# Values made with tokens on the partitions, four heads at a time, in a hybrid decoder trunk; the first two gates each moved one place forward

## The chip, the core and the metric

The kernel runs on one core of one Trainium2 chip. The metric is the device time of one execution in microseconds (us). TensorE is the engine of the matmuls, VectorE, ScalarE and GpSimd work on tiles, SyncE issues most of the transfers. In the rows they are PE, DVE, ACT, POOL and SP; PEld is TensorE's weight load, and "SPq" and "ACTq" are transfers issued by SyncE and ScalarE.

## The reference

Two layers over 256 tokens of width 2048, all float32. Each layer has three branches that are mixed by gates, and a SwiGLU block behind them.

```python
proj = einsum('bld,de->ble', x, w_in[l]) + b_in[l]
q_sb, k_sb, v_sb, u_ssm, q_mem, gate_logits = split(proj, ...)   # 1024, 1024, 1024, 512, 512, 3 x 2048
sb    = stick_breaking_attention(q_sb, k_sb, v_sb)               # 8 heads of 128
p_sb  = sb @ sb_w_out[l]
g     = gelu(s5(u_ssm, ...));  a, b = split(g @ ssm_w_glu[l])
p_ssm = (a * sigmoid(b)) @ ssm_w_out[l]
p_mem = memory_attention(q_mem, mem, mem_w_kv[l]) @ mem_w_out[l]
gates = sigmoid(gate_logits)                                     # three gates of 2048
merged = gates[0] * p_sb + gates[1] * p_ssm + gates[2] * p_mem
x = layer_norm(ALPHA * x + merged @ w_o[l])
x = layer_norm(ALPHA * x + (silu(x @ w_gate) * (x @ w_up)) @ w_down)
```

For one head the attention takes weights w_t (tokens by tokens, through a sigmoid and a running product) and multiplies them with v; the matmul needs v with the key tokens on the partitions.

## The kernel before

**Precision and chunks.** Each float32 operand is split into a high part (fp32r) and the rest: `hi` is a ScalarE copy of a loaded weight (L736), `lo` a VectorE subtraction of the two (L1206). A product is hi*hi + lo*hi + hi*lo. Weights come in chunks of 1 MB (128 x 2048), in four `raw` slots filled by SyncE, and are split in halves of 128 x 1024 into four `hi` and four `lo` slots. A half's slot is free when TensorE has done the half four places back (`half_done`). Chunks are numbered through the whole program, by the table PHASES: U (the first states of a layer), BR (three branch turns of 10 chunks), BL (the last turn, 6 chunks), GLU (18), G (three merge groups of 16), WO, F0, FB, FL. On ScalarE and VectorE `split_next` (L739, L1209) stands for each chunk c and splits chunk c + 1, so both engines' queues are an order written out by hand, with their other work between.

**Two forms of product.** `product` (L1822) makes one 128-wide output with the output's columns on the partitions: a 128 x 128 block of weights is stationary, and x streams past, 512 columns (hi and lo of 256 tokens) for the hi weights (L1829), 256 for the lo weights (L1832), 16 times in a chunk. The result is [head column, token]; ScalarE takes its first 256 columns (`first_half`, L753), VectorE adds the second 256 (`take`, L1215). `group_half` (L1867) has tokens on the partitions: a block of x is stationary and 512 columns of weights stream past, three times for each block (L1854 to L1856), for two blocks of tokens, 24 matmuls in a chunk; four chunks make 512 output columns in two banks.

**A branch turn** (L2002 on TensorE, L917 on ScalarE, L1447 on VectorE) has two attention heads, one memory head and 128 SSM channels. Its chunks are q, k, v of the first head (0, 1, 2), q, k, v of the second (3, 4, 5), and k, v of the memory, u and q of the memory for the next turn (6 to 9). Between them stand small float32 products: `state_inputs` (L2019), the memory scores (L2099), z, tri, `attend` (L2071) and `state_outputs`. A scan over time runs on VectorE (`scan_states`), ten steps for each of two pairs, and ends in `state_outputs`. `v_turn` (L2064) transposes v of a head (k = 0 and 2, source v_f) and of the memory (k = 1, source vm_f) by two 128 x 128 transposes each (L2068); ScalarE copies the result (`copy_v`, L953) to v_s or vm_s. In the first turn of layer 0 eight tables are transposed as well and saved to DRAM (`table`), and ScalarE waits for these saves before it goes on to the output of the first head. Set-up work for the SSM runs on GpSimd until about that turn.

**The last turn and the merge.** In BL the places of chunks 6 to 9 are taken by the four chunks of the first gate (`first_gate`, L1995), into banks 2 and 3. Then come the GLU products in four steps t = 0 to 3 (`glu_blocks`, L2190) into the banks of GLU_BANK, steps 0 and 1 first without their last quarter, which waits for the last GELU. Then TensorE does the sb products (two chunks, banks 2 and 3), gate 1 (four chunks, banks 0 and 1), ssm (one chunk, banks 2 and 3 again), gate 2 (four chunks, banks 4 and 5) and mem (one chunk, banks 6 and 7). VectorE adds a gate's bias to its logits (`gate_logits`, L1619), ScalarE does a tanh, and VectorE's `merge(b)` multiplies the branch by it (L1630 for b = 0). Before ssm, TensorE waits for merge(0), which reads banks 2 and 3, and for the GLU's last result:

```python
branch_products("GLU", 0, GLU_SPANS, 0)                                  # L2223
pe.wait_ge(tile_out, tile_no("GLU", l, 0, 7) + 1 + TILE_CREDIT)
gate_products("GLU", 0, GLU_SPANS, 1)
pe.wait_ge(merge_step, 20 * l + 1)
pe.wait_ge(glu_lo, 4 * l + 4)
branch_products("GLU", 0, GLU_SPANS, 1)                                  # L2228
```

On VectorE merge(0) comes in the loop at L1685 behind `split_next("GLU", l, 0, 8)`, that is, behind both lo halves of chunk 9. Ahead of the first norm of each layer TensorE runs matmuls whose result nobody reads (L2297), and sixteen of that kind on ident (L1914) at the program's start.

## Time and profile before

| | |
|---|---|
| median of 3 runs | 2956.91 us (2956.4 to 2957.02) |
| profiled execution | 2957.04 us |
| its span | 2955.3 us (1.7 us lie around it) |
| TensorE, VectorE, ScalarE busy | 99%, 65%, 46% of the span |
| mean rate of the transfers | 192 GB/s |
| chain that ended last | 97% TensorE |

In the timeline a row is: start, duration, engine, line, operation, output <- input, shapes, count; in brackets the idle time ahead of it and what ended it. An x2 row holds two instructions. Starts of TensorE are measured, ends are modelled: a matmul's cost in a stream is the distance from its start to the next one's. In the view of waits a row gives who waited for whom, the total, the times and the longest, in us.

### The profile page before, as it was taken

To read this page: it belongs to the slowest core of one execution; us is meant where nothing else is said; L and a number is where in the kernel's file an instruction comes from. 1 tells how busy PE (TensorE), PEld (TensorE's weight loads), DVE (VectorE), ACT (ScalarE), POOL (GpSimd) and SP (SyncE) were. 2 spreads that over 40 slices of the span, in tenths; PEclk is the share of its full clock that TensorE was granted. 3 is DMA by queue.
4 is the path that set the end of the run, shared out by engine and by line. 5 is a ranking of instruction groups with operands and counts; after the bars stand their busy time and mean duration, and the time that the engine had idled before them with its cause. 6 is when DMAs were issued, how large, how long until landed. Compare 5 with 4: busy or idle time off the path is not lost.

```text
span 2955.3 us, 37621 instructions
## 1 busy us (share of the span) xinstructions
PE 2935.8 (99%) x14068; PEld 2449.7 (83%) x14068; DVE 1932.0 (65%) x2754; ACT 1371.5 (46%) x1646; POOL 46.6 (2%) x117
## 2 busy tenths in 40 slices
PE   8999999999999999999999999999999999999999
PEld 7888888888888888888888888888888888888887
DVE  8899755555755555555699996555666555555556
ACT  6656544444544444444466554444444444444443
POOL 5000000000000000000000000000000000000000
PEclk9999999999999999999999999999999999999999
DMA  9666565656655555555556565665656555555554
GB/s 252 194 189 179 198 205 194 207 190 212 229 191 192 187 196 185 194 189 190 191 140 170 161 188 195 203 202 198 223 172 213 185 194 189 188 195 185 189 194 142
DMA packets 390020, 568.31 MB, mean 192 GB/s; under 512 B 20408, under 2 KB 194592, under 8 KB 389024
## 3 DMA queue, kind: packets, MB, share of 16 engines
q1 hardware_dynamic: 385712, 554.77, 58.5%
q10 hardware_dynamic: 4208, 12.21, 1.1%
q8 instruction: 62, 1.02, 0.1%
q14 instruction: 38, 0.31, 0.0%
HBM read 558.81 MB, written 8.13 MB: 192 GB/s over the span
## 4 chain that ended last, share of the span: by engine, by line
PE 97%; DVE 1%; ACT 1%; DMA 0%; issue 0%; SPq 0%; ACTq 0%; DVEq 0%
PE banks L1854 26%; PE banks L1856 26%; PE banks L1855 26%; PE banks L1829 9%; PE banks L1832 4%; PE banks L1844 1%; PE banks L2275 1%; PE banks L2209 1%; PE banks L2297 0%; DMA raw<-in_w_in 0%; DVE lo L1206 0%; PE banks L1846 0%; PE banks L2028 0%; PE banks L2040 0%; PE banks L2210 0%
## 5 line engine op out<-in xcount | busy, mean ns | idle before, releaser
L1206 DVE TENSOR_TENSOR lo<-raw,hi 128x1024 fp32r<-128x1024 f32 x1014 | 1232.0, 1225 | 957.5 <-ACT hi L736 870.6
L736 ACT ACTIVATE hi<-raw 128x1024 fp32r<-128x1024 f32 x932 | 977.8, 1059 | 1163.1 <-PE banks L1856 1155.1
L1854 PE MATMUL banks<-hi,xs 128*128 128x512 f32 x2176 | 852.0, 392 | 2.4 <-DVE xs L1349 2.4
L1856 PE MATMUL banks<-hi,xs 128*128 128x512 f32 x2176 | 847.3, 389 | 0.0
L1855 PE MATMUL banks<-lo,xs 128*128 128x512 f32 x2176 | 846.9, 389 | 0.0
L1854 PEld LDWEIGHTS banks<-hi,xs 128*128 128x128 f32 x2176 | 408.5, 188 | 86.6 <-DVE xs L1349 2.9
L1856 PEld LDWEIGHTS banks<-hi,xs 128*128 128x128 f32 x2176 | 408.4, 188 | 85.2
L1855 PEld LDWEIGHTS banks<-lo,xs 128*128 128x128 f32 x2176 | 408.7, 188 | 82.9
L1829 PE MATMUL banks<-xs,hi 128*128 128x512 f32 x960 | 307.1, 401 | 0.5 <-DVE lo L1206 0.5
L1854 PE MATMUL banks<-hi,hT 128*128 128x512 f32 x704 | 274.1, 389 | 0.0
L1856 PE MATMUL banks<-hi,hT 128*128 128x512 f32 x704 | 273.9, 389 | 0.0
L1855 PE MATMUL banks<-lo,hT 128*128 128x512 f32 x704 | 273.9, 389 | 0.0
L1832 PEld LDWEIGHTS banks<-xs,lo 128*128 128x128 f32 x960 | 180.3, 188 | 42.6
L1832 PE MATMUL banks<-xs,lo 128*128 128x256 f32 x960 | 189.2, 278 | 0.0
L1856 PEld LDWEIGHTS banks<-hi,hT 128*128 128x128 f32 x704 | 132.1, 188 | 27.4
L1854 PEld LDWEIGHTS banks<-hi,hT 128*128 128x128 f32 x704 | 132.1, 188 | 27.4
L1855 PEld LDWEIGHTS banks<-lo,hT 128*128 128x128 f32 x704 | 132.2, 188 | 27.3
L1829 PEld LDWEIGHTS banks<-xs,hi 128*128 128x128 f32 x960 | 146.9, 189 | 5.9 <-issue 5.5
L748 ACT ACTIVATE hi<-raw 128x1024 fp32r<-128x1024 f32 x80 | 83.9, 1059 | 106.2 <-PE banks L1856 106.2
L1410 DVE TENSOR_TENSOR rows<-rows,banks 128x1024 f32<-128x1024 f32 (+1 forms) x98 | 109.2, 1147 | 3.3 <-PE banks L1856 3.3
L1854 PE MATMUL banks<-hi,mT 128*128 128x512 f32 x256 | 99.8, 390 | 0.0
L1856 PE MATMUL banks<-hi,mT 128*128 128x512 f32 x256 | 99.6, 389 | 0.0
(254 smaller groups left out, 2430.5 us busy)
## 6 DMA issues: line engine op xcount, KB each, us to landing
raw<-in_ffn_w_gate_up SPq DMA_DIRECT2D x176, 1024.0 KB, 5.0
raw<-in_w_in SPq DMA_DIRECT2D x156, 1024.0 KB, 5.2
raw<-in_ffn_w_down SPq DMA_DIRECT2D x88, 1024.0 KB, 4.9
raw<-in_w_o SPq DMA_DIRECT2D x32, 1024.0 KB, 5.0
raw<-in_sb_w_out SPq DMA_DIRECT2D x16, 1024.0 KB, 5.0
raw<-in_mem_w_kv SPq DMA_DIRECT2D x12, 1024.0 KB, 5.8
raw<-in_ssm_w_out SPq DMA_DIRECT2D x8, 1024.0 KB, 5.1
raw<-in_mem_w_out SPq DMA_DIRECT2D x8, 1024.0 KB, 5.1
```

The lines of the kernel that those rows point to most:

```text
L736: act.activation(hi[:, hl_slot(ph, c, h), :], raw[:, slot, h * HALF:(h + 1) * HALF], ACT.Copy).then_inc(hi_ready, 1)
L748: act.activation(hi[:, hl_slot(ph, c + 1, h), :], raw[:, slot, h * HALF:(h + 1) * HALF], ACT.Copy).then_inc(hi_ready, 1)
L1206: dve.tensor_tensor(lo[:, s, :], raw[:, slot, h * HALF:(h + 1) * HALF], hi[:, s, :].bitcast(F32), ALU.subtract).then_inc(lo_ready, 1)
L1410: dve.tensor_tensor(y2, y2, src, ALU.add).then_inc(rows_out, 1)
L1829: pe.matmul(dst[:, :], hi[:, s, k * P:(k + 1) * P], x_t[:, k0 + k, :], start=first and k == 0, stop=False)
L1832: ins = pe.matmul(dst[:, 0:T], lo[:, s, k * P:(k + 1) * P], x_t[:, k0 + k, 0:T], start=False, stop=last and k == 7)
L1844: pe.matmul(bank[base + j], hi[:, s, at[j]], x_t[:, k, :], start=k == 0, stop=False)
L1854: pe.matmul(dst, xh, hi[:, s, w], start=first, stop=False)
L1855: pe.matmul(dst, xh, lo[:, s, w], start=False, stop=False)
L1856: return pe.matmul(dst, xl, hi[:, s, w], start=False, stop=last)
L2209: pe.matmul(dst[:, :], hi[:, s, w], gT[:, k, :], start=k == 0, stop=False)
L2275: ins = pe.transpose(bank[base + q][:, k * T + m * P:k * T + (m + 1) * P], silu[:, m, (2 * q + k) * P:(2 * q + k + 1) * P], ident[:])
```

## The change

v of four heads is made at once in the second form, with tokens on the partitions: the first four heads' v by four chunks at the end of U (c = 4 to 7), the other four's in places 2 and 5 of turns 0 and 1, where v's chunks stood. VectorE's new `v_rows` adds the bias out of banks 2 and 3 into v_first or v_last, which `attend` reads. v_turn is left for vm_f alone; passes and takes for v go. In places 2 and 5 of turns 2 and 3 the first gate is made, in BL's last places the second gate, and the GLU phase has no gate 1 between sb and ssm. Banks change (BU, tables, GLU_BANK), and some set-up work moves behind U's new chunks. On SyncE, ScalarE and VectorE the order follows. The diff, cut; its hunks are those of the order tables, SyncE, ScalarE, VectorE and TensorE.

```diff
-    "U": (1, [0, 1, 2, 3], [2] * 4),
+    "U": (1, [0, 1, 2, 3] * 2, [2] * 4 + [1] * 4),
...
-    "GLU": (1, ([2, 3, 0, 1] * 5)[:18], [1] * 4 + [4] * 2 + [1] * 12),
+    "GLU": (1, ([2, 3, 0, 1] * 4)[:14], [1] * 4 + [4] * 2 + [1] * 8),
...
-GLU_SPANS = {"gate0": 0, "glu": 4, "sb": 6, "gate1": 8, "ssm": 12, "gate2": 13, "mem": 17}
+GLU_SPANS = {"gate1": 0, "glu": 4, "sb": 6, "ssm": 8, "gate2": 9, "mem": 13}
...
-GLU_BANK = (0, 1, 4, 5, 6, 7, 0, 1)
+GLU_BANK = (4, 5, 6, 7, 4, 5, 6, 7)
+TILE_AT = {0: 0, 1: 1, 3: 2, 4: 3, 6: 4, 7: 5, 8: 6, 9: 7}
+WIDE_AT = (2, 5)
...
-        BU, Z, S, VO, Y = (bank[2], bank[3], bank[4], bank[6]), bank[4], bank[5], bank[6], bank[7]
+        BU, Z, S, VO, Y = (bank[5], bank[4], bank[6], bank[7]), bank[4], bank[5], bank[6], bank[7]
...
+                for c in range(4):
+                    load_block("U", 0, 4 + c, w, 4 * c, 2 * SBW)
+                    if l == 0 and c == 1:
+                        load_ssm_rest()
+                if l == 0:
+                    sp.wait_ge(par_T, 1)
+                else:
+                    sp.wait_ge(v_ready, 2 * l)
+                load_v_bias(0)
...
+                    cols = [(w, t * 256), (w, t * 256 + SBW), None, (w, t * 256 + P), (w, t * 256 + SBW + P), None]
...
+                        if at is None:
+                            load_block(ph, i, c, w, 4 * (2 * (t % 2) + WIDE_AT.index(c)),
+                                       2 * SBW + GROUP if t < 2 else GATE_COLS)
+                        else:
+                            load(ph, l, i, c, columns(*at))
+                    if t == 0:
+                        sp.wait_ge(v_ready, 2 * l + 1)
+                        load_v_bias(1)
...
-                for c in range(4):
-                    load_gate_block("GLU", 0, GLU_SPANS, 0, 1, c)
-                    if c == 0:
-                        sp.wait_ge(attn_done, 12 * l + 15)
-                        load_bias(0, 1)
+                sp.wait_ge(attn_done, 12 * l + 15)
+                load_bias(0, 1)
                 load_branch("GLU", 0, GLU_SPANS, 0, 1)
-                sp.wait_ge(gate_in, 12 * l + 1)
-                load_bias(0, 2)
                 for c in range(4):
                     load_gate_block("GLU", 0, GLU_SPANS, 0, 2, c)
+                    if c == 2:
+                        sp.wait_ge(gate_in, 12 * l + 1)
+                        load_bias(0, 2)
                 load_branch("GLU", 0, GLU_SPANS, 0, 2)
...
+                split_next("U", l, 0, 4)
                 for k, col in enumerate((None, None, bias_col(l, 24), bias_col(l, 28))):
                     first_half("U", l, 0, k, bank[U_BANK[l][k]], done("U", l, 0, 1 if l and k < 2 else 3), col)
-                    if l == 0 and k == 1:
-                        b_blocks(0, 4)
+                split_next("U", l, 0, 5)
+                if l == 0:
+                    c_blocks(0, 1)
+                split_next("U", l, 0, 6)
+                if l == 0:
+                    b_blocks(0, 4)
+                split_next("U", l, 0, 7)
...
-                    tile(2, turn * 2 + 16)
...
-                    copy_v(0, VO, v_s, 3)
...
+                    def v_rows(g, dst, ready):
+                        dve.wait_ge(half_done, ready)
+                        dve.wait_ge(v_bias_in, 16 * (2 * l + g + 1))
+                        dve.tensor_tensor(dst[:].rearrange("p h m d -> p m h d"),
+                                          banks[:, 2:4, :].rearrange("p m (h d) -> p m h d", d=P),
+                                          v_bias[:].rearrange("p a (h d) -> p a h d", d=P)
+                                          .broadcast_to([P, TT, 4, P]), ALU.add).then_inc(v_ready, 1)
...
+                    if turn == 0:
+                        v_rows(0, v_first, chunk_no(ph, l, i, 0) * 2 + HALF_CREDIT)
...
-                    tile(2, v_f)
...
+                        if turn == 1:
+                            v_rows(1, v_last, chunk_no(ph, l, i, 6) * 2 + HALF_CREDIT)
...
-                for c in range(7, 18):
+                for c in range(7, 14):
                     split_next("GLU", l, 0, c)
                     if c == 8:
                         merge(0, 4 * l, upto("GLU", 0, 8))
-                    if c == 12:
-                        gate_logits(1, 4 * l, GATE_BANK[1], upto("GLU", 0, 12))
+                        gate_logits(1, 4 * l, GATE_BANK[1], upto("GLU", 0, 4))
+                    if c == 9:
+                        merge(1, 4 * l, upto("GLU", 0, 9))
                     if c == 13:
-                        merge(1, 4 * l, upto("GLU", 0, 13))
-                    if c == 17:
-                        gate_logits(2, 4 * l, GATE_BANK[2], upto("GLU", 0, 17))
+                        gate_logits(2, 4 * l, GATE_BANK[2], upto("GLU", 0, 13))
...
+                for c in range(4):
+                    for h in range(2):
+                        k = 4 * c + 2 * h
+                        group_half("U", l, 0, 4 + c, h, xs, k, 2, k == 0, k == KD - 2)
...
-                def first_gate(c):
+                def second_gate(c):
                     if c == 0:
-                        pe.wait_ge(bu_copied, 16 * l + 18)
+                        pe.wait_ge(tile_out, tile_no("GLU", l, 0, 0) + TILE_CREDIT)
                     for h in range(2):
                         k = 4 * c + 2 * h
-                        group_half("GLU", l, 0, c, h, xs, k, 2, k == 0, k == KD - 2)
+                        group_half("GLU", l, 0, c, h, xs, k, GATE_BANK[1], k == 0, k == KD - 2)
...
+                    def wide(c):
+                        at = 2 * (turn % 2) + WIDE_AT.index(c)
+                        if at == 0:
+                            pe.wait_ge(v_ready, 2 * l + 1 + turn // 2)
+                        for h in range(2):
+                            k = 4 * at + 2 * h
+                            group_half(ph, l, i, c, h, xs, k, 2, k == 0, k == KD - 2)
...
+                        pe.wait_ge(gelu_step, n * 5 + 1)
...
                     got(-1)
+                    pe.wait_ge(bu_copied, n * 4 + 3)
                     for t in range(TT):
                         ins = pe.matmul(S[:, t * T:(t + 1) * T], qm_f[:, t * P:(t + 1) * P], km_f[:], start=True,
                                         stop=True)
                     ins.then_inc(s_done, 1)
                     gemm(1, xs)
-                    gemm(2, xs)
+                    wide(2)
...
-                    v_turn(0, v_f, VO)
...
+                    vm_turn()
+                    wide(5)
...
-                    v_turn(2, v_f, VO)
...
                     if ks[0] == 0:
                         if t == 0:
-                            pe.wait_ge(tile_out, tile_no("GLU", l, 0, 0) + TILE_CREDIT)
-                        elif t == 1:
                             pe.wait_ge(w_ready, 8 * (l + 1) + 1)
                             pe.wait_ge(o_lo, 12 * (l + 1))
-                        elif t == 2:
+                        elif t == 1:
                             pe.wait_ge(o_lo, 12 * (l + 1) + 1)
                             pe.wait_ge(gelu_step, (4 * l + 3) * 5 + 6)
                         else:
-                            pe.wait_ge(tile_out, tile_no("GLU", l, 0, 1) + 1 + TILE_CREDIT)
+                            pe.wait_ge(tile_out, tile_no("GLU", l, 0, 2 * t - 3) + 1 + TILE_CREDIT)
...
                 pe.wait_ge(tile_out, tile_no("GLU", l, 0, 7) + 1 + TILE_CREDIT)
-                gate_products("GLU", 0, GLU_SPANS, 1)
                 pe.wait_ge(merge_step, 20 * l + 1)
                 pe.wait_ge(glu_lo, 4 * l + 4)
                 branch_products("GLU", 0, GLU_SPANS, 1)
```

## Rows read from the trace of the kernel before

**Rows 1.** The page's first part, TensorE: busy us, share, count; VectorE and ScalarE behind.

```profile
PE 2935.8 (99%) x14068; PEld 2449.7 (83%) x14068; DVE 1932.0 (65%) x2754; ACT 1371.5 (46%) x1646; POOL 46.6 (2%) x117
```

**Rows 2.** The waits of TensorE over the span: total us, times, longest.

```profile
PE banks L2133 <- ACT vm_s L956: 1.4, 1, 1.4
PE banks L1992 <- ACT b_blk L831: 1.0, 1, 1.0
PE banks L1992 <- ACT stage L913: 0.8, 2, 0.5
...
PE banks L1829 <- DVE lo L1206: 0.5, 1, 0.5
```

**Rows 3.** TensorE's timeline in the last branch turn of layer 0.

```profile
262.60 0.63 PE L1829 MATMUL banks<-xs,hi 128*128 128x512 f32 x2
...
268.17 0.59 PE L2048 MATMUL banks<-q_f,k_f 128*128 128x256 f32 x2
...
269.30 0.71 PE L1829 MATMUL banks<-xs,hi 128*128 128x512 f32 x2
...
274.97 0.38 PE L2068 MATMUL banks<-ident,v_f 128*128 128x128 f32 x2
275.19 0.60 PE L2058 MATMUL banks<-sp_t,ntri 128*128 128x256 f32 x2
...
289.70 0.48 PE L1854 MATMUL banks<-hi,xs 128*128 128x512 f32 x1
...
295.27 0.38 PE L2068 MATMUL banks<-ident,v_f 128*128 128x128 f32 x2
```

**Rows 4.** The timeline of all engines in the GLU products of layer 0.

```profile
319.79 0.66 ACT L759 ACTIVATE tmp<-banks 128x256 f32<-128x256 f32 x2 [0.38 <-PE banks L2210]
...
320.21 0.76 DVE L1219 SCALAR_TENSOR_TENSOR glu<-banks,tmp 128x256 f32<-128x256 f32 x2 [1.89 <-ACT tmp L759]
320.30 0.40 PE L2209 MATMUL banks<-gT,hi 128*128 128x512 f32 x1
```

**Rows 5.** The timeline of all engines near the end of a branch turn (the third).

```profile
242.23 1.12 DVE L1496 SCALAR_TENSOR_TENSOR scan<-scan,pw,scan_t 128x127 f32<-128x127 f32 x4
...
245.39 0.85 PE L2040 MATMUL banks<-scan,tab 128*32 128x256 f32 x12
```

**Rows 6.** The timeline of all engines at the end of the sb products of layer 0.

```profile
336.89 0.39 PE L1854 MATMUL banks<-hi,xs 128*128 128x512 f32 x1
337.10 1.06 ACT L736 ACTIVATE hi<-raw 128x1024 fp32r<-128x1024 f32 x1 [1.60 <-PE banks L1856]
...
338.19 1.23 DVE L1206 TENSOR_TENSOR lo<-raw,hi 128x1024 fp32r<-128x1024 f32 x1 [1.16 <-ACT hi L736]
...
339.33 1.21 DVE L1630 SCALAR_TENSOR_TENSOR acc<-gate,banks 128x1024 f32<-128x1024 f32 x1
```

**Rows 7.** TensorE's timeline over the ssm chunk of layer 0: its first, the next chunk's first.

```profile
358.66 0.39 PE L1854 MATMUL banks<-hi,ssmT 128*128 128x512 f32 x1
...
364.10 0.39 PE L1854 MATMUL banks<-hi,xs 128*128 128x512 f32 x1
```

**Rows 8.** The timeline of all engines in the first branch turn of layer 0.

```profile
43.53 0.63 PE L1829 MATMUL banks<-xs,hi 128*128 128x512 f32 x2
...
50.73 1.13 PE L2099 MATMUL banks<-km_f,qm_f 128*128 128x256 f32 x4
50.81 1.08 ACT L934 ACTIVATE scan<-banks 128x512 f32<-128x512 f32 x2 [1.95 <-PE banks L2028]
...
52.96 2.01 ACT L736 ACTIVATE hi<-raw 128x1024 fp32r<-128x1024 f32 x2 [0.69 <-DMA raw<-in_w_in]
```

**Rows 9.** TensorE's timeline at the program's start, the warming matmuls.

```profile
4.28 3.41 PE L1914 MATMUL banks<-ident 128*128 128x128 f32 x16
...
8.40 1.95 PE L1914 MATMUL banks<-ident 128*128 128x128 f32 x16
```

**Rows 10.** Busy time in a stretch: engines, then granted clock (PEclk), DMA share, GB/s.

```profile
88.00:92.00 4.00, 2.55 (x14) 2.08 (x13) 3.79 (x17) 1.02 (x3) 0.00 (x0) 1.00 0.72 204
```

More of the change, by code:

```diff
@@ L52 @@
 ORDER = ["U", "BR", "BL", "GLU", "G", "WO", "F0", "FB", "FL"]
-TILES = {"U": 4, "BR": 10, "BL": 6, "GLU": 8, "G": 0, "WO": 0, "F0": 0, "FB": 0, "FL": 0}
+TILES = {"U": 4, "BR": 8, "BL": 4, "GLU": 8, "G": 0, "WO": 0, "F0": 0, "FB": 0, "FL": 0}
 def _bases(per_turn):
@@ L155, in trunk @@
         region = ExitStack()
+        ahead = sb("ahead", [P, 6, 2 * T], stack=region)
+        v_last = sb("v_last", [P, 4, 2, P], stack=region)
+        region.close()
+        region = ExitStack()
         b_nat = sb("b_nat", [P, 2, 32, GC], stack=region)
@@ L184, in trunk @@
         k_f = sb("k_f", [P, T], stack=region)
-        v_f = sb("v_f", [P, T], stack=region)
+        gel_y = sb("gel_y", [P, T], stack=region)
         qm_f = sb("qm_f", [P, T], stack=region)
@@ L454, in branch_turn @@
                                  (w, (t + (3 * SBW // P + 1)) * P), (w, (t + ((3 * SBW + SSMW) // P + 1)) * P)]
-                    for c, (src, col) in enumerate(cols):
-                        load(ph, l, i, c, columns(src, col))
-                        if first and c == 1:
-                            load_ssm_rest()
+                    for c, at in enumerate(cols):
+                        if at is None:
[6 more added lines that the diff above has]
+                        load_v_bias(1)
                 if l == 0:
@@ L494, in _ @@
                 for c in range(4):
-                    load_gate_block("GLU", 0, GLU_SPANS, 0, 0, c)
+                    load_gate_block("GLU", 0, GLU_SPANS, 0, 1, c)
                     if c == 1:
@@ L926, in tile @@
                             bias = bias_col(l, bias_tile)
-                        first_half(ph, l, i, c, bank[c % 2], done(ph, l, i, c), bias, scale)
-                        if l == 0 and turn == 1 and c % 2 and c < 8:
-                            save_mem(c // 2)
+                        k = TILE_AT[c]
+                        first_half(ph, l, i, k, bank[k % 2], done(ph, l, i, c), bias, scale)
+                        if l == 0 and turn == 1 and k % 2:
+                            save_mem(k // 2)
                     def copy_bu(j):
@@ L1027, in branch_turn @@
                     out_hi(0, VO, sbT[:, bass.ds(turn * 2, 1), 0:T])
-                    copy_v(1, S, vm_s, 2)
-                    tile(5, turn * 2 + 17)
+                    copy_vm()
                     softplus(1)
@@ L1454, in tile @@
                     def tile(c, dst, scale=1.0):
-                        take(ph, l, i, c, bank[c % 2], dst[:], scale)
+                        k = TILE_AT[c]
+                        take(ph, l, i, k, bank[k % 2], dst[:], scale)
+                    def v_rows(g, dst, ready):
[5 more added lines that the diff above has]
+                                          .broadcast_to([P, TT, 4, P]), ALU.add).then_inc(v_ready, 1)
                     def scan_states(pair, first, last_):
@@ L1647, in _ @@
                 split_next("GLU", l, 0, 4)
-                gate_logits(0, 4 * l, 2, upto("GLU", 0, 4))
+                gate_logits(0, 4 * l, 2, upto("GLU", 0, 0))
                 def glu_take(t):
@@ L1684, in _ @@
                 dve.wait_ge(glu_lo, 4 * l + 4)
-                for c in range(7, 18):
+                for c in range(7, 14):
                     split_next("GLU", l, 0, c)
@@ L2062, in tri, with vm_turn @@
                                   skip_group_check=True).then_inc(tri_done, 1)
-                    def v_turn(k, src, o):
-                        pe.wait_ge(v_copied, n * 3 + (k + 1))
+                    def vm_turn():
+                        pe.wait_ge(v_copied, n + 1)
                         for t in range(2):
-                            ins = pe.transpose(o[:, t * P:(t + 1) * P], src[:, t * P:(t + 1) * P], ident[:])
+                            ins = pe.transpose(S[:, t * P:(t + 1) * P], vm_f[:, t * P:(t + 1) * P], ident[:])
                         ins.then_inc(vt_done, 1)
@@ L2073, in attend @@
                         pe.wait_ge(w_ready, n * 2 + (e + 2))
-                        pe.wait_ge(v_copied, n * 3 + (2 + 2 * e))
+                        pe.wait_ge(v_ready, 2 * l + 1 + turn // 2)
                         pe.wait_ge(o_lo, n * 3 + (e + 1))
-                        pe.matmul(VO[:, T:2 * T], v_s[:, 0, :], w_t[:, 0:T], start=True, stop=False)
-                        pe.matmul(VO[:, T + P:2 * T], v_s[:, 1, :], w_t[:, T:384], start=False, stop=True
+                        v, at = (v_first, v_last)[turn // 2], (2 * turn + e) % 4
+                        pe.matmul(VO[:, T:2 * T], v[:, at, 0, :], w_t[:, 0:T], start=True, stop=False)
+                        pe.matmul(VO[:, T + P:2 * T], v[:, at, 1, :], w_t[:, T:384], start=False, stop=True
                                   ).then_inc(attn_done, 1)
@@ L2092, in branch_turn @@
                         pe.wait_ge(tab_b_full, n * 16)
-                    got(-2)
+                    got(-1 if turn == 0 else -2)
                     state_inputs()
```

152 lines of the change are left out of this document (70 added, 82 removed).

## The prediction, made before the change was run

> **What bounds the kernel now.** The page comes first: TensorE is busy 2935.8 us of a span of 2955.3 us, VectorE 65% and ScalarE 46% of it [rows 1]. So every microsecond that TensorE issues counts, and work of the other engines counts only where TensorE waits for it. The view of TensorE's waits shows how little there is to win besides: in the part that the change touches they are 1.4 us for vm_s, 1.0 us for b_blk, 0.8 us for the table copies and 0.5 us for a lo half [rows 2]; all fall into the first branch turn of layer 0. The later branch turns have none. The change is therefore an account of TensorE's own instructions, plus the places where it sets TensorE next to work that used to be hidden. The timeline of one engine has to be read by its starts: the ends are modelled, so the cost of a matmul is the distance to the next start.
>
> **Part 1, the transposes of v, taken out.** A turn of one head's v starts at 274.97 us and the next work at 275.19 us [rows 3]: 0.22 us. There are two in a turn (k = 0 and 2 of v_turn), and 2 layers have 8 turns, so there are 16 of them: 16 x 0.22 = 3.5 us saved. All of it is on TensorE and on the path. With them go, for each head, a 256-wide pass and a copy on ScalarE and a take of about 0.38 us on VectorE (0.76 us for two such [rows 4]). I cost these at nothing: TensorE hides them, and nothing in a steady turn waits for those engines. What comes late next would be the scan: VectorE's last step ends at 242.23 + 1.12 = 243.35 us and TensorE reads it at 245.39 us [rows 5], 2.0 us of room. TensorE's turn gets about 0.7 us shorter, VectorE loses two takes, and in turns 0 and 1 it gains v_rows, a 1024-wide add out of two banks, nearest to the 1.21 us of the merge step [rows 6]. Room left: 2.0 - 0.7 + 0.8 - 1.2 = 0.9 us, so still no wait. In turn 1 v_rows stands ahead of scan steps and a take for km_f, in turn 0 behind the split of the second chunk and ahead of the scan; both queues have work of TensorE's of a whole chunk before they are needed.
>
> **Part 2, the products for v.** The number of columns is the same. A head in the old form streams 16 x (512 + 256) columns, 12288; a chunk in the new form streams 24 x 512, 12288 too, and layer by layer 8 chunks stand for 8. The form has a price, though. An old chunk runs from 262.60 to 268.17 us, 5.57 us; behind fp32 work from 269.30 to 274.97, 5.67 us [rows 3]. A chunk in the new form takes 364.10 - 358.66 = 5.44 us [rows 7], and behind fp32 work 295.27 - 289.70 = 5.57 us [rows 3]. That is 0.13 and 0.10 us less; half of the 16 chunks stand in either place: 8 x 0.13 + 8 x 0.10 = 1.8 us saved. The first gate's four chunks move into turns 2 and 3, the second gate's into the last turn, in the form that they have: nothing.
>
> **Part 3, the GLU banks.** Step t = 2 gets banks 4 and 5, which step t = 0 has just filled, where before it had free ones. It must wait until both halves are taken. Before, ScalarE starts on them at 319.79 us and VectorE's two takes run from 320.21 for 0.76 us, to 320.97 us, while TensorE starts step 2 at 320.30 us [rows 4]. So TensorE waits 0.67 us and a semaphore's way: 0.7 us, twice: 1.4 us lost. Step 3's banks are taken by the time it comes.
>
> **Part 4, the second gate no longer stands between the sb and the ssm products.** Both write banks 2 and 3, so the ssm products wait for merge(0), as before. But before, 4 chunks of the second gate covered it; now there is nothing between. What stands ahead of merge(0) on VectorE stays: the split of the chunk after next. Its second half needs the hi slot that the last sb half frees. The trace of before shows this very sequence with TensorE busy elsewhere: the matmul behind the last one of sb starts at 336.89 us; ScalarE begins the hi half at 337.10, VectorE the lo half at 338.19 and merge(0) at 339.33 us for 1.21 us [rows 6]. It is over at 340.54 us, 3.65 us after 336.89. With the way to TensorE 3.7 us, once a layer: 7.4 us lost. The lower end is merge alone, behind sb at once: 1.3 us a layer; the order in VectorE's queue rules it out, and I take 3.7. ssm also waits for glu_lo, done long before under the two sb chunks. The second logits and the tanh come behind merge(0) and are not waited for until the G loop, 5 chunks on. SyncE's queue: the ssm load now stands behind the wait for the last attention product and one bias load, the third bias load inside gate 2's loads; both conditions hold before the slots come free.
>
> **Part 5, the start of layer 0.** Four wide chunks (21.8 us) now run at 43.53 us [rows 8], ahead of the first branch chunk, and give the set-up time. The waits for the lo half (0.5 us) and for b_blk (1.0 us) [rows 2] lie behind a late VectorE and go; of the table copies' 0.8 us I let 0.3 go, since ScalarE has one pass less before them. The vm_s wait hangs on ScalarE waiting for a table save to land; I leave it. Saved 1.8 us. Two costs stand against it. The states now fill bank 5 first, which the memory scores need: the scores start at 50.73 us, while ScalarE's first two copies start at 50.81 us and take 1.08 us for both [rows 8], so the scores would wait for the first until about 51.35: 0.6 us, in this turn alone (elsewhere a half chunk lies between). And the third v chunk takes the place in SyncE's queue of the chunk that ScalarE had to wait for, until 52.96 us [rows 8]. The hi half takes 1.0 us of that 2.01 us pair and the lo half as long as that between 338.19 and 339.33 [rows 6], 1.2 us with its end, so it would be ready at about 55.2 us, while TensorE arrives at 43.53 + 2 x 5.44 = 54.4 us: 0.8 us at most, nothing if the wider rows land sooner; I take 0.4. Net: -1.8 + 0.6 + 0.4 = -0.8 us, bounds -3.7 (all four waits of [rows 2] gone, no cost) and +1.5.
>
> **Sum.** -3.5 - 1.8 + 1.4 + 7.4 - 0.8 = +2.7 us. The profiled execution took 2957.04 us, its span plus 1.7; the median of the runs is 2956.91. So 2956.9 + 2.7 = 2959.6 us, 0.09% above before. About 0.2%, 5.9 us, is what a measurement of this kernel can tell from no change.
>
> **Rivals.**
> 1. Slower: the clock falls in the new gap. Nothing in the trace of before, once it is under way, shows TensorE idle for as long as 3.7 us. At the start it shows both paces: the first 16 warming matmuls on ident take 3.41 us from end to end, the same 16 later 1.95 us [rows 9], about half the pace, the 1.2 GHz level against 2.4. One such slow stretch behind the gap costs 3.41 - 1.95 = 1.5 us, one twice as long 3 us; two layers, 3 to 6 us: 2962.6 to 2965.6. From 1.6 us a gap on, the whole is 0.2% slower. For it: the code puts matmuls that compute nothing ahead of each layer's first norm. Against it: the 1.4 us wait of [rows 2] passes without loss; the granted clock stays at 1.00 around it [rows 10]. Chance 0.14. The Trainium skill ("TensorE: Matmul & The Clock Gate", section "Why this matters for your kernels") speaks against this change here: it warns of idle gaps between bursts of matmuls, after which the clock is back at half. By that rule the gap would be followed by a slow stretch; no row of before has a gap to test it on.
> 2. The start of layer 0 is short of data: the third and fourth v chunks land 2 to 3 us late because the small SSM loads sit ahead of them. Then 2961.5 to 2963. For it: ScalarE already waits for that load [rows 8]. Chance 0.10.
> 3. The extra 21.8 us wipe out all waits of the first turn (-3.7 in place of -0.8): 2956.7. For it: VectorE and ScalarE start that turn with nothing behind. Against: the table copies and the save of the tables depend on the turn's own order. Chance 0.10.
> 4. The change doesn't do what part 4 says: merge(0) comes sooner, 1.3 us a layer. Then 2959.6 - 4.8 = 2954.8; with rival 3 as well 2951.9. For it only that the queue might run ahead if the halves were split earlier; the semaphores say otherwise. Chance 0.05.
>
> **How the numbers follow.** The forecast itself has 0.58 (its own range 2957.8 to 2961.9: the upper bound of part 5 above, some of the lower below); 0.03 stays for something unseen. Slower by over 0.2% needs 2962.8: most of rival 1, the end of rival 2 and half of the unseen, 0.16. Faster by over 0.2% needs 2951.0: rivals 3 and 4 together and more, 0.04. The rest, 0.80, is within. The range reaches down to rival 3 and a little of 4, up into the middle of rival 1: 2955.5 to 2964.0.
>
> **What would show it.** In the profile after: no transposes of v_f and 32 fewer fp32 records of them; branch turns 0.7 us shorter; in both layers one TensorE wait of about 3.6 us for VectorE's merge step between sb and ssm, and one of about 0.7 us in the GLU for its take; scores of layer 0's first turn 0.6 us late. The forecast is wrong if the merge wait is under 3 us, if matmuls behind it start 0.45 us apart instead of 5.44 / 24 = 0.23, or if the stretch up to the first turn's end differs from the sum by more than 2 us.

## The result and the profile after

The changed kernel takes 2962.58 us (median, 2961.1 to 2964.91), the kernel before 2956.76 us (2956.3 to 2957.4): ratio 1.002, 95% interval 1.0013 to 1.0027, 5.8 us more. Forecast were 2959.6 us, 2.7 us more in the prediction's own sum, with a range up to 2964.0. The time lies in the range, but above the forecast's own part of it (2957.8 to 2961.9), where rival 1, the clock, begins. The profiled execution took 2963.30 us, so its sums can be set against the 2957.04 us of the profile of before: +6.3 us.

The page's line for TensorE answers to [rows 1]. Busy time is nearly the same with 160 instructions fewer, and the span is longer:

```profile
PE 2936.3 (99%) x13908; PEld 2444.0 (83%) x13908; DVE 1930.4 (65%) x2742; ACT 1359.9 (46%) x1614; POOL 47.8 (2%) x117
```

TensorE's waits after (total us, times, longest) answer to [rows 2]. New are the wait ahead of ssm (L1879, 3.6 us in each layer), the one for the GLU's take (L2245) and the scores' wait for the first state copy (L2142). Gone are b_blk and the 0.5 us for a lo half; vm_s and the tables have shrunk.

```profile
PE banks L1879 <- issue: 7.2, 2, 3.6
...
PE banks L2245 <- DVE glu L1235: 1.3, 2, 0.6
PE banks L2174 <- ACT vm_s L977: 0.9, 1, 0.9
...
PE banks L2142 <- ACT scan L955: 0.8, 1, 0.8
...
PE banks L2023 <- ACT stage L933: 0.3, 1, 0.3
```

The gap itself, layer 0: TensorE's timeline (start, us, ..., idle time before it in brackets).

```profile
355.65 0.39 PE L1881 MATMUL banks<-hi,sbT 128*128 128x512 f32 x1
359.62 0.47 PE L1879 MATMUL banks<-hi,ssmT 128*128 128x512 f32 x1 [3.58 <-issue]
...
360.65 0.63 PE L1879 MATMUL banks<-hi,ssmT 128*128 128x512 f32 x1
...
363.57 0.40 PE L1880 MATMUL banks<-lo,ssmT 128*128 128x512 f32 x1
```

VectorE's and ScalarE's timelines in the same gap answer to [rows 6]: hi half, lo half, merge(0), in the forecast order.

```profile
357.16 1.23 DVE L1222 TENSOR_TENSOR lo<-raw,hi 128x1024 fp32r<-128x1024 f32 x1 [1.43 <-ACT hi L765]
358.30 1.22 DVE L1656 SCALAR_TENSOR_TENSOR acc<-gate,banks 128x1024 f32<-128x1024 f32 x1
...
356.07 1.06 ACT L765 ACTIVATE hi<-raw 128x1024 fp32r<-128x1024 f32 x1 [1.60 <-PE banks L1881]
```

The next matmul could have started at 355.88 us and started at 359.62 us: 3.74 us, against 3.7 forecast. But behind the gap the matmuls start 0.43 us apart where 0.23 is usual, until 363.57 us. The windows show the granted clock (the column behind POOL):

```profile
355.00:360.00 5.00, 1.42 (x7) 0.90 (x6) 3.44 (x4) 1.06 (x1) 0.00 (x0) 1.00 0.73 225
360.00:365.00 5.00, 5.00 (x17) 3.96 (x16) 0.87 (x1) 1.76 (x2) 0.00 (x0) 0.66 0.56 198
365.00:370.00 5.00, 5.00 (x24) 4.14 (x23) 3.18 (x3) 1.68 (x3) 0.00 (x0) 1.00 0.00 0
```

About double the distance, at a granted clock of 0.66 over that window, is the 1.2 GHz level in place of 2.4. Ten matmuls take 363.57 - 359.62 = 3.95 us; at full pace the same ten take 2.37 us (run x4 below), so this costs 1.6 us. Layer 1 shows the same gap and 1.5 us of loss. That is rival 1. There is a third such stretch in the set-up, behind two gaps of 0.77 and 0.85 us:

```profile
20.21 0.41 PE L1933 MATMUL banks<-ident,rows 128*128 128x128 f32 x2 [0.77 <-DVE xs L1271]
21.47 0.71 PE L1869 MATMUL banks<-xs,hi 128*128 128x512 f32 x2 [0.85 <-DVE lo L1222]
...
22.60 1.20 PE L1869 MATMUL banks<-xs,hi 128*128 128x512 f32 x2
...
24.31 1.20 PE L1869 MATMUL banks<-xs,hi 128*128 128x512 f32 x2
...
25.81 0.70 PE L1869 MATMUL banks<-xs,hi 128*128 128x512 f32 x2
```

Before has gaps of 0.82 and 1.14 us at the same place, and no slow stretch behind them:

```profile
21.91 0.70 PE L1844 MATMUL banks<-xs,hi 128*128 128x512 f32 x2 [1.14 <-DVE lo L1206]
...
24.67 0.70 PE L1844 MATMUL banks<-xs,hi 128*128 128x512 f32 x2
```

The three steps from 21.47 to 25.81 us take 4.34 us in after, the same three from 21.91 to 24.67 us 2.76 in before: again 1.6 us.

**The rest of the account.** Branch turns are told from the start of their state inputs. First two of them in before (layer 0), then two in after (layer 1; from the second turn on the distance is the same in both layers):

```profile
186.42 1.15 PE L2028 MATMUL banks<-u_f,tab 32*128 32x256 f32 x16
...
252.19 1.15 PE L2028 MATMUL banks<-u_f,tab 32*128 32x256 f32 x16
```

```profile
1537.24 1.15 PE L2069 MATMUL banks<-u_f,tab 32*128 32x256 f32 x16
...
1602.33 1.15 PE L2069 MATMUL banks<-u_f,tab 32*128 32x256 f32 x16
```

They are 65.77 us apart before and 65.09 after. That is 0.68 us a turn for parts 1 and 2 together; the forecast was 0.44 + 0.23. From the first turn's state inputs to the third's it takes 205.89 - 72.55 = 133.34 us after and 186.42 - 49.65 = 136.77 us before: 3.43 us less, of which 1.36 are two turns of parts 1 and 2. So part 5 brings 2.1 us there, not 0.8. Ahead of the first turn nothing is gained: its state inputs start 72.55 - 49.65 = 22.90 us later, which is 21.8 us for the four wide chunks and 1.6 us for the slow stretch, less 0.4 us by which TensorE was earlier at 21.47 us.

### The profile page after: what moved, and what is told of

The parts are those of the page before. It is cut to its first block, busy times and chain, and to the rows that moved or that the text cites. A ratio compares the mean times of both kernels' runs of the same rounds, so it can differ in the third digit from the quotient of the medians.

```text
span 2961.6 us, 37199 instructions
## 1 busy us (share of the span) xinstructions
PE 2936.3 (99%) x13908; PEld 2444.0 (83%) x13908; DVE 1930.4 (65%) x2742; ACT 1359.9 (46%) x1614; POOL 47.8 (2%) x117
## 4 chain that ended last, share of the span: by engine, by line
PE 98%; DVE 1%; issue 0%; ACT 0%; DMA 0%; SPq 0%; ACTq 0%
PE banks L1879 27%; PE banks L1881 27%; PE banks L1880 27%; PE banks L1854 7%; PE banks L1857 3%; PE banks L1869 1%; PE banks L2310 1%; PE banks L2245 0%; PE banks L2332 0%; PE banks L1871 0%; DMA raw<-in_w_in 0%; PE banks L2069 0%; PE banks L2081 0%; PE banks L2174 0%; PE banks L2246 0%
## 5 line engine op out<-in xcount | busy, mean ns | idle before, releaser
L1879 PE MATMUL banks<-hi,xs 128*128 128x512 f32 x2304 | 902.6, 392 | 2.5 <-DVE xs L1360 2.5
L1881 PE MATMUL banks<-hi,xs 128*128 128x512 f32 x2304 | 897.1, 389 | 0.0
L1880 PE MATMUL banks<-lo,xs 128*128 128x512 f32 x2304 | 896.6, 389 | 0.0
L1879 PEld LDWEIGHTS banks<-hi,xs 128*128 128x128 f32 x2304 | 432.6, 188 | 90.9 <-DVE xs L1360 2.9
L1881 PEld LDWEIGHTS banks<-hi,xs 128*128 128x128 f32 x2304 | 432.4, 188 | 90.5
L1880 PEld LDWEIGHTS banks<-lo,xs 128*128 128x128 f32 x2304 | 432.7, 188 | 87.5
L1879 PE MATMUL banks<-hi,hT 128*128 128x512 f32 x704 | 274.0, 389 | 0.0
L1854 PE MATMUL banks<-xs,hi 128*128 128x512 f32 x704 | 226.0, 402 | 0.0
L1857 PEld LDWEIGHTS banks<-xs,lo 128*128 128x128 f32 x704 | 132.2, 188 | 31.2
L1879 PEld LDWEIGHTS banks<-hi,hT 128*128 128x128 f32 x704 | 132.1, 188 | 27.3
L1857 PE MATMUL banks<-xs,lo 128*128 128x256 f32 x704 | 138.7, 278 | 0.0
L1854 PEld LDWEIGHTS banks<-xs,hi 128*128 128x128 f32 x704 | 108.1, 189 | 5.4 <-issue 4.8
L1879 PE MATMUL banks<-hi,mT 128*128 128x512 f32 x256 | 99.8, 390 | 0.0
```

What stands on the lines that cost most here:

```text
L1854: pe.matmul(dst[:, :], hi[:, s, k * P:(k + 1) * P], x_t[:, k0 + k, :], start=first and k == 0, stop=False)
L1857: ins = pe.matmul(dst[:, 0:T], lo[:, s, k * P:(k + 1) * P], x_t[:, k0 + k, 0:T], start=False, stop=last and k == 7)
L1879: pe.matmul(dst, xh, hi[:, s, w], start=first, stop=False)
L1880: pe.matmul(dst, xh, lo[:, s, w], start=False, stop=False)
L1881: return pe.matmul(dst, xl, hi[:, s, w], start=False, stop=last)
```

## The experiments

Unless told otherwise each is the changed kernel with the edit shown.

**x1, merge(0) ahead of the second lo half.**

```diff
@@ VectorE, chunk 8 of the GLU phase
-split_next("GLU", l, 0, 8)
-merge(0, 4 * l, upto("GLU", 0, 8))
+branch_weights(9, 0)
+merge(0, 4 * l, upto("GLU", 0, 8))
+branch_weights(9, 1)
```

> The changed kernel, with VectorE's order changed at one place of each layer: between the sb and the ssm products it does the lo half that is ready early, then merge(0), and the second lo half only behind it. Theory (the gap between sb and ssm is 3.58 us because merge(0) stands behind the second lo half, and its length is what makes TensorE's clock fall to half behind it): the gap becomes merge alone, 1.3 us, and no matmul behind it starts 0.43 us after the one before; per layer 2.3 us of gap and 1.7 us of slow matmuls go: 2962.6 - 2 x 4.0 = 2954.6 us. Rival (the slow matmuls have another cause, such as the banks being read or the load of other engines there): the gap shrinks but the slow stretch stays: 2962.6 - 2 x 2.3 = 2958.0 us.

Measured: 2955.12 us (2953.97 to 2956.23), 0.9994 of before (0.9985 to 1.0003). TensorE's timeline in layer 0 and 1 of x1:

```profile
357.68 0.47 PE L1883 MATMUL banks<-hi,ssmT 128*128 128x512 f32 x1 [1.36 <-issue]
357.99 0.40 PE L1884 MATMUL banks<-lo,ssmT 128*128 128x512 f32 x1
...
1815.40 0.47 PE L1883 MATMUL banks<-hi,ssmT 128*128 128x512 f32 x1 [1.36 <-issue]
```

The gap is merge alone and behind it the pace is 0.23 us at once. Of the 7.5 us gained 2 x 2.2 are gap; 3.0 are left for the clock, 1.5 a layer. The theory's 2954.6 us came, the rival's 2958.0 did not. So the order in VectorE's queue makes the length of the gap, as part 4 said, and the clock's loss goes with it.

**x2 and x7, the gap filled with idle matmuls.** Its length for the data stays; only TensorE's idleness changes. (x7: range(8).)

```diff
@@ TensorE, between the sb and the ssm products
 pe.wait_ge(tile_out, tile_no("GLU", l, 0, 7) + 1 + TILE_CREDIT)
+for k in range(15):
+    pe.matmul(bank[4][:, :], ident_r[:], xs[:, k, :], start=True, stop=True)
 pe.wait_ge(merge_step, 20 * l + 1)
```

> The changed kernel, with 15 matmuls of 512 columns that compute nothing, on a free bank, put on TensorE into each layer's gap between sb and ssm. 15 x 0.227 = 3.4 us, less than the gap of 3.58 us, so the ssm products still start when merge(0) is done. Theory (idle time lowers the clock): the wait for merge(0) is down to about 0.2 us, the ssm products start at the same distance from sb as before, but 0.23 us apart at once: -1.7 us a layer, 2962.6 - 3.4 = 2959.2 us. Rival (something else slows the matmuls behind the gap): 0.43 us apart still, no gain: 2962.6 us.

> Run x2_fill_gap with 8 idle matmuls in place of 15: after them TensorE idles for 3.58 - 8 x 0.227 = 1.8 us until merge(0) is done. Theory A (any gap that long lowers the clock): the ssm products start 0.43 us apart for a while, 2962.6 us or 0.5 us less. Theory B (a gap of under 2 us is too short to lower it in most executions): as with 15 matmuls, 2959.0 us. If it happens in some executions only, the runs have two heights, 1.7 us apart for each layer in which the clock fell.

Measured: x2 2958.99 us (2958.31 to 2960.64), ratio 1.0008 (0.9999 to 1.0017); x7 2959.01 us (2958.16 to 2960.33), ratio 1.0009 (1.0000 to 1.0018). First x2's timeline around the gap, then its window:

```profile
354.52 0.39 PE L1881 MATMUL banks<-hi,sbT 128*128 128x512 f32 x1
354.74 3.66 PE L2262 MATMUL banks<-xs,ident_r 128*128 128x512 f32 x15
358.45 0.50 PE L1879 MATMUL banks<-hi,ssmT 128*128 128x512 f32 x1
...
360.00:365.00 5.00, 5.00 (x24) 4.14 (x23) 1.23 (x1) 2.70 (x3) 0.00 (x0) 1.00 0.35 136
```

and x7's:

```profile
357.61 0.50 PE L1879 MATMUL banks<-hi,ssmT 128*128 128x512 f32 x1 [1.68 <-DVE acc L1656]
357.94 0.40 PE L1880 MATMUL banks<-lo,ssmT 128*128 128x512 f32 x1
```

x2 is the run that tells the clock from everything else. Products, banks, loads and the merge are where they were, the time between the last sb and the first ssm matmul is the same (358.45 - 354.52 = 3.93 us, in after 3.97), and work that computes nothing brings 3.6 us: 3.4 were forecast. By the medians eight idle matmuls do as well as fifteen, and in both layers of x7's profile 1.68 us of idleness left the clock as it was. That it always does is not shown: x7's executions have two heights, five from 2958.16 to 2958.69 us and five from 2959.96 to 2960.33, at a mean granted clock of 0.999 in place of 1.000. Its expectation named this as the sign of a clock that falls in some of them. But x2, x3 and x9 have such upper executions too, three of eleven each, without that gap; the set-up's stretch makes them as well, and no profile of x7 caught an upper one. The Trainium skill ("TensorE: Matmul & The Clock Gate", section "Why this matters for your kernels") tells to avoid idle gaps between bursts of matmuls, since the clock drops behind them; for the gaps of 3.58 us in after these two runs agree, and layer 0 of x4 below has the same gap without the fall.

**x3, the second gate between sb and ssm.**

```diff
-GLU_SPANS = {"gate1": 0, "glu": 4, "sb": 6, "ssm": 8, "gate2": 9, "mem": 13}
+GLU_SPANS = {"gate1": 0, "glu": 4, "sb": 6, "gate2": 8, "ssm": 12, "mem": 13}
@@ TensorE
+gate_products("GLU", 0, GLU_SPANS, 2)
 pe.wait_ge(merge_step, 20 * l + 1)
 pe.wait_ge(glu_lo, 4 * l + 4)
 branch_products("GLU", 0, GLU_SPANS, 1)
-gate_products("GLU", 0, GLU_SPANS, 2)
@@ VectorE
-if c == 9:
-    merge(1, 4 * l, upto("GLU", 0, 9))
 if c == 13:
-    gate_logits(2, 4 * l, GATE_BANK[2], upto("GLU", 0, 13))
+    merge(1, 4 * l, upto("GLU", 0, 13))
+    gate_logits(2, 4 * l, GATE_BANK[2], upto("GLU", 0, 12))
@@ SyncE: the load of ssm behind those of gate2
```

> The changed kernel, with the second gate's four chunks (now its loads, splits and products too) put between the sb and the ssm products in each layer, as the first gate's four once were; merge(1) and the second gate's logits come together behind the ssm products. Theory: four chunks of 5.44 us cover merge(0), the gap of 3.58 us and the slow stretch of 1.7 us both go and nothing new waits, since turn_merged comes two chunks into the G loop: 2962.6 - 2 x 5.3 = 2952.0 us, faster than before by 0.16%. Rival (the later merge(1), logits and tanh, about 10 us of VectorE work behind ssm with the splits, are late for the transposes of the merged rows): up to 3 us a layer come back, 2958 us.

Measured: 2951.39 us (2950.65 to 2952.84), 0.9982 of before (0.9973 to 0.9991). TensorE passes from gate 2 to ssm without a pause:

```profile
376.28 0.39 PE L1880 MATMUL banks<-hi,xs 128*128 128x512 f32 x1
376.51 0.39 PE L1878 MATMUL banks<-hi,ssmT 128*128 128x512 f32 x1
```

So the changed kernel takes 5.4 us less than before once this one edge in the order of its products is mended, and that edge cost it 11.2 us, more than all of its loss. Three of the eleven executions stand 1.1 to 1.5 us above the median, as in x2.

**x4 and x8, part 1 put back.** The 16 pairs of transposes, on the identity: in x4 in the changed kernel, in x8 in x2.

```diff
@@ TensorE, attend(e), behind its waits
+for t in range(2):
+    pe.transpose(VO[:, t * P:(t + 1) * P], ident[:], ident[:])
 pe.matmul(VO[:, T:2 * T], v[:, at, 0, :], w_t[:, 0:T], start=True, stop=False)
```

> The changed kernel, with two transposes of the identity put back ahead of each head's product of weights and v, 16 pairs in all: TensorE issues what the old form's transposes of v were, nobody waits for them. Theory (a pair costs TensorE 0.22 us, nothing covers it): 2962.6 + 16 x 0.22 = 2966.1 us, branch turns 0.44 us longer than 65.09 us. Rival (a part of them was under waits or overlaps with the work around it, so that taking them out brought less): under 1.8 us more, 2964.4 us or less.

> Run x2_fill_gap with the 16 pairs of transposes of x4_transposes_back. With the gaps filled the clock cannot fall in them, so the price of the pairs stands alone. Theory: 2959.0 + 16 x 0.22 = 2962.5 us, and the runs lie closer together than the 6.3 us between the lowest and the highest of x4. Rival (the pairs themselves make the 2969 us of x4, by a clock that falls elsewhere or by work around them that comes late): over 2965 us again.

Measured: x4 2968.91 us (five executions: 2963.13, 2965.09, 2968.91, 2969.26, 2969.39), ratio 1.0037 (1.0023 to 1.0050); x8 2961.65 us (2961.36 to 2963.79), ratio 1.0018 (1.0009 to 1.0028). State inputs of two turns of layer 1, in x8:

```profile
1537.24 1.15 PE L2069 MATMUL banks<-u_f,tab 32*128 32x256 f32 x16
...
1602.72 1.15 PE L2069 MATMUL banks<-u_f,tab 32*128 32x256 f32 x16
```

65.48 us against the 65.09 of after: 0.39 us for two pairs, 3.1 us for 16, and x8's median stands 2.7 us above that of x2. Part 1 is real and a little smaller than 3.5. The pairs stand ahead of another product than the old ones did, so for the old ones this is an estimate. x4 missed: the clock makes its sum unreadable. Its profiled execution (2965.09 us) shows what part chance has. First the gap of layer 0, then that of layer 1:

```profile
361.26 0.47 PE L1879 MATMUL banks<-hi,ssmT 128*128 128x512 f32 x1 [3.58 <-issue]
...
363.63 0.39 PE L1880 MATMUL banks<-lo,ssmT 128*128 128x512 f32 x1
...
1822.76 0.47 PE L1879 MATMUL banks<-hi,ssmT 128*128 128x512 f32 x1 [3.58 <-issue]
1823.06 0.39 PE L1880 MATMUL banks<-lo,ssmT 128*128 128x512 f32 x1
...
1824.49 0.63 PE L1879 MATMUL banks<-hi,ssmT 128*128 128x512 f32 x1
```

The same 3.58 us pass without loss in one layer and lower the clock in the other, there 1 us after work has begun again. Three of its executions take 2969 us; their mean granted clock is 0.997, against 0.998 in the profiled one and 0.999 in the fastest, so they lost more to the clock. Where, no profile caught; that stays open. With the gaps filled (x8) it did not occur in 11.

**x5, free banks for step 2 of the GLU** (on x3).

```diff
-GLU_BANK = (4, 5, 6, 7, 4, 5, 6, 7)
+GLU_BANK = (4, 5, 6, 7, 2, 3, 4, 5)
@@ TensorE: step 2 waits for the first gate's logits, step 3 for tile 1, sb for tile 5
```

> Run x3_gate2_ahead_of_ssm with one more edit: the GLU's step 2 writes banks 2 and 3, free since the first gate's logits were taken, and step 3 writes 4 and 5; the sb products wait for the takes of step 2. Theory (TensorE's wait of 0.65 us in each layer is for the banks that step 0 still holds): both waits go, nothing new, 2951.4 - 1.3 = 2950.1 us. Rival (VectorE is late itself, so the same 0.65 us show up at the sb products, which now wait for its takes of step 2): 2951.4 us.

Measured: 2951.64 us (2951.11 to 2953.81), ratio 0.9984 (0.9975 to 0.9993), no gain. Its waits:

```profile
PE banks L1878 <- DVE glu L1235: 1.9, 2, 1.0
```

The rival held, and a bit more: 0.65 us at step 2 are gone, 0.97 us stand at the sb products. With these banks TensorE waits for VectorE's chain of takes, products and halves in the GLU all the same. The 1.4 us of part 3 were sized rightly, but this choice of banks does not avoid them.

**x6, x9, x10: the start, and ScalarE's wait for saved tables.** x6 adds to x5, x10 to x9, six idle matmuls around the two gaps of the set-up; x9 adds to x3 the earlier copy of vm_s.

```diff
@@ TensorE, set-up, step 8 (x6, x10)
+keep_awake(3)
 early_turn(k + 4)
+keep_awake(3)
@@ ScalarE, first turn of layer 0 (x9, x10)
 if first:
+    copy_vm()
     for q in range(5):
         act.wait_ge(tab_saved[q], 32 if q < 2 else 16)
     act.wait_ge(bu_done, n * 4 + 4)
     load_tables(n + 1, 0, tab_b_full)
 out_hi(0, VO, sbT[:, bass.ds(turn * 2, 1), 0:T])
-copy_vm()
+if not first:
+    copy_vm()
```

> Run x5_free_glu_banks with six matmuls on ident that compute nothing, three ahead of each of the two idle gaps of 0.8 us in the set-up, at 19.4 and 20.6 us, where some profiles (after, x1, x4) show TensorE at half its clock from 22 to 25 us and others (before, x2, x3) do not. Theory (those gaps set off the slow stretch in some executions: 3 to 5 of 11 runs stand 1.5 to 2 us above the rest): the upper runs go, all lie within 1 us, the median falls by 0 to 0.7 us: 2949.4 to 2950.1. Rival (it has another cause): the runs keep their two heights, the median stays at that of x5 or is up to 0.5 us more.

Measured: x6 2954.25 us (2951.33 to 2955.27), ratio 0.9989 (0.9979 to 0.9998): neither theory, it is 2.6 us slower than x5. Its profile shows full pace at 22 us, but a longer wait for vm_s with a slow stretch behind it (the pairs take 1.20 us, 0.63 usual):

```profile
110.88 1.15 PE L2177 MATMUL banks<-probT,vm_s 128*128 128x256 f32 x4 [2.16 <-ACT vm_s L977]
...
113.29 1.20 PE L1853 MATMUL banks<-mT,hi 128*128 128x512 f32 x2
...
115.68 0.62 PE L1853 MATMUL banks<-mT,hi 128*128 128x512 f32 x2
```

ScalarE's timeline of x6 shows where the wait is from: ScalarE stands idle for 4.85 us (3.57 in x5) before the output at 110.17 us, waiting to load tables that have to be saved first, and the copy to vm_s is behind. Why that takes 1.3 us longer than in x5 is open. Seven executions of x6 lie at 2953.0 to 2955.3 us, four at 2951.3 to 2952.0, near the median of x5.

```profile
109.79 0.34 ACTq L861 DMA_DIRECT2D tab<-tab_save  x1
110.17 0.38 ACT L982 ACTIVATE sbT<-banks 128x256 fp32r<-128x256 f32 x1 [4.85 <-issue]
110.45 0.38 ACT L977 ACTIVATE vm_s<-banks 128x256 f32<-128x256 f32 x1
```

> Run x3_gate2_ahead_of_ssm with ScalarE's copy of vm_s moved, in layer 0's first branch turn alone, ahead of its wait for the saved tables and the load of them. Theory (TensorE's wait for vm_s, 0.9 us in x3 and 2.2 us in x6, is ScalarE standing in its queue before a save that has not landed): the wait goes, the load of the tables has a whole turn of room: 2951.4 - 0.9 = 2950.5 us. Rival (what stands behind, the sb output and the next soft step, comes later by as much and TensorE waits there instead): 2951.4 us.

> Run x9_vm_copy_first with the six idle matmuls of x6 in the set-up. In x6 the profile shows no slow stretch at 22 us, but one at 113 us behind a vm_s wait of 2.2 us, so its upper runs need not be due to the start. With that wait gone as well: theory (idle gaps of the start set off the slow stretch there): all runs within about 1 us of their median, which is 0 to 0.7 us under that of x9. Rival (the start's slow stretch has another cause): two heights again, some 1.7 us apart.

Measured: x9 2949.82 us (2949.43 to 2951.66), ratio 0.9977 (0.9968 to 0.9986); x10 2949.84 us (2949.57 to 2950.42), ratio 0.9976 (0.9967 to 0.9985). In x9 no wait for vm_s is left, and nothing takes its place: 1.6 us under x3, more than the 0.9 us of x3's profile. Eight of its executions lie within 0.6 us, three up to 2.2 us above the lowest; its own profile has the slow stretch of the start (window first, then the matmuls), x10's has not:

```profile
20.00:25.00 5.00, 3.56 (x15) 3.04 (x15) 4.11 (x7) 2.87 (x7) 4.99 (x14) 0.73 1.14 329
...
23.18 1.20 PE L1870 MATMUL banks<-xs,hi 128*128 128x512 f32 x2
```

```profile
20.00:25.00 5.00, 4.28 (x29) 3.72 (x28) 4.13 (x8) 2.97 (x7) 4.92 (x14) 1.00 1.14 329
...
22.85 0.71 PE L1870 MATMUL banks<-xs,hi 128*128 128x512 f32 x2
```

All eleven executions of x10 lie within 0.85 us. The theory's narrow spread came, the rival's two heights did not: none of eleven executions against three of eleven. That fits short idle gaps that set off the third slow stretch in some executions and six idle matmuls that keep it away, but eleven executions a side are few. The median gains nothing, since most executions never had the stretch. x9 and x10 are the fastest versions found, 0.24% under before.

**x11 and x12, the kernel before,** with the six idle matmuls of the set-up (the same diff), and as it is.

> The kernel before, with the six idle matmuls of x6 and x10 in the set-up, nothing else. Its runs show no two heights, yet about two in five of them have a mean granted clock of 0.999 in place of 1.000, and these stand only 0.4 us above the others. Theory (the slow stretch at the start occurs in the kernel before as often as after, but there its 1.6 us shorten the 3.7 us of waits of the first branch turn, which the change has taken away): all runs now show 1.000, the median is 2956.6 us, 0 to 0.3 us less than before. Rival (the 0.999 has nothing to do with the start): two in five runs still show 0.999.

> The kernel before, unchanged, for one more profile of it. With a chance of two in five it shows the slow stretch at 22 us; then the theory of x11 wants its matmuls 0.43 us apart there, the waits of the first branch turn for b_blk, the tables and vm_s shorter by about as much as the stretch cost, and the second branch turn's start as in the first profile within 0.5 us. Otherwise it shows how far two profiles of one kernel lie apart.

Measured: x11 2955.92 us (2955.21 to 2956.16), 0.9996 of before (0.9987 to 1.0005); ten of its eleven executions have a mean clock of 1.000, nearly as the theory said. But the time is lower than forecast, and by another way: its wait for vm_s is 0.3 us in place of the 1.4 of [rows 2].

```profile
PE banks L2137 <- ACT vm_s L956: 0.3, 1, 0.3
```

x12 took 2957.39 us at a mean clock of 0.999, and shows full pace in the set-up:

```profile
22.70 0.70 PE L1844 MATMUL banks<-xs,hi 128*128 128x512 f32 x2
...
24.54 0.70 PE L1844 MATMUL banks<-xs,hi 128*128 128x512 f32 x2
```

So a mean clock of 0.999 is no sign of the slow stretch. The mean also counts the end of the span, where TensorE has no work left: from 2952.0 to 2955.3 us the granted clock is 0.60 in x12 and 0.63 in before, and a little of that decides how the mean is rounded. The theory that the waits of the first turn hid such a stretch in the kernel before is thus not borne out by either run. Whether it occurs there at all is open; no profile of before caught it.

## Why the prediction was right, and where it was not

**The bound** was right: 99% of TensorE, and every difference found lies in its own instructions, its waits or its clock.

**Parts 1 and 2** were right as a sum: 0.68 us a turn against 0.44 + 0.23. Part 1 was 0.39 us a turn (x8), not 0.44, which leaves an estimated 0.29 for part 2 in place of 0.23. Over 8 turns they give -5.4 us; -5.3 was forecast.

**Part 3** was right: the view of waits has 1.3 us (L2245) against +1.4. By the distance of starts, which is how part 4 is counted, it is 0.8 us a layer, +1.6: the matmul at 339.26 us could have started at 338.46. x5 shows that the cause named, banks still in use, is only the nearer one; with other banks TensorE waits for VectorE a little later.

**Part 4** was right in place, order and length: 3.74 us in each layer against 3.7, +7.5 in all. x1 and x3 show it from both sides.

**Part 5** was too cautious: -0.8 forecast, -2.1 measured between the first and the third turn. The scores' wait (0.76 us, forecast 0.6) came; the 0.4 us for a late third v chunk did not; and vm_s, left at 1.4, fell to 0.9 in the profiled execution. x11 and x6 show this wait at 0.3 and 2.2 us where the same kernels without six idle matmuls of the set-up have 1.4 and 0.9, so a forecast to a tenth was not to be had.

**The step that failed** is the likeliest case itself: "Against it: the 1.4 us wait of [rows 2] passes without loss". That row says nothing of a gap 2.5 times as long, and the text said in the same breath that no row of before has such a gap. The sum gave the clock nothing; the runs show 3.1 us for the two gaps. Its chance of 0.14 was too low, and of the forecast's three signs of being wrong the second came: matmuls 0.43 us apart behind the gap. Without the clock the terms as measured sum to -5.4 + 1.6 + 7.5 - 2.1 = +1.6 us, 2958.6 us from the 2957.04 of the profiled execution; x2's profiled execution, whose granted clock fell neither in the gaps nor in the set-up, took 2958.92. The clock puts 1.6 + 1.5 us on top for the two gaps and in the profiled execution 1.6 us in the set-up: 2963.3 us, and 2963.30 were measured. That the time lies in the range is in part luck: part 5 was wrong by 1.3 us the other way, and with it as forecast the median would be 2963.9 us, at the end of the range. The slow stretch in the set-up, which no term and no rival had, adds to this in some executions. The rival itself was priced well: 1.5 us for a slow stretch, from [rows 9].

The other rivals: the start of layer 0 was not short of data, the first turn gained 2.1 us net and not 3.7, and merge(0) came no sooner.

By the bound of 0.2% the result lies at the edge, 0.197% over before.

## What to carry over

When work that covered a wait is moved away, price the wait by everything that stands ahead of it in the releasing engine's queue, and then price what the idle time does to TensorE's clock: here 3.58 us of waiting cost another 1.5 to 1.6 us in three of the four gaps profiled. If the trace has no gap of that length, the clock is no side case; it deserves a large share of the chances, because the nearest row speaks only for its own, shorter gap. Before accepting such a gap look for independent products to put into it (x3), then for a shorter queue ahead of the release (x1), and last for idle matmuls (x2), which bring back the clock alone.

## What was not expected of the hardware

The length of a gap does not decide alone. Behind 1.36 us (x1, both layers), 1.45 us (before) and 1.68 us (x7, both layers) the granted clock stayed full; behind 2.16 us it fell in x6; behind 3.58 us it fell in three of the four gaps profiled in after and x4 and not in the fourth. In the set-up it fell behind 0.77 and 0.85 us in after, and not behind 0.77 and 1.39 us in x3, which has the same set-up. Nearly the same work can therefore show it or not from one execution to the next. The spread fits that: 3.8 us in after, with a mean clock of 0.999 or 0.998 in nineteen executions and 0.997 in the slowest, and 0.9 us in x10, which has no gap of 3.58 us and the idle matmuls in the set-up.

What sorts the profiles of the set-up is not the gaps but how early TensorE had come to full pace among the warming matmuls. In after, x1, x4, x8 and x9 that was at 8.0 to 8.8 us, and all five have the slow stretch; in before, x2 and x5 it was by 7.6 us and in x3 and x12 at 10.0 us or later, and none has it. x7 is the exception, at 8.8 us and without it. The three profiles with the six idle matmuls (x6, x10, x11) came to full pace at 9.4 to 9.5 us, so they test neither side; only x10's spread speaks for those matmuls.

Each of the three slow stretches in the profile of after cost 1.5 to 1.6 us, in the set-up as behind the gaps.
